# Two fused transformer blocks on one core: 256-column strips joined into 416 and 512 columns, a row statistic moved earlier, vector 6 turned one row sooner

## What is computed

```python
def first_block(x, c, ...):
    mod = (silu(c) @ w_ada + b_ada).reshape(b, 3, 3, D_MODEL)      # nine vectors of 1024
    x = x + 0.5 * mod[:, 0, 2] * swiglu(modulate(x, ...), w13[0], w2[0])
    h = modulate(x, norm_w[1], mod[:, 1, 0], mod[:, 1, 1])
    proj = h @ w_in                      # columns 0:416 are c_q (256), c_kv (128), k_rope (32)
    ...                                  # attention, convolution, two gated branches
    x = x + mod[:, 1, 2] * y
    h = modulate(x, norm_w[2], mod[:, 2, 0], mod[:, 2, 1])         # mod[:, 2, 0] is vector 6
    x = x + 0.5 * mod[:, 2, 2] * swiglu(h, w13[1], w2[1])
    return x

def second_block(x, ...):
    h = rmsnorm(x, norm_mix_g)
    z = h @ w_in                         # qa 1024, ka 256, va 256, qb, kb, vb 768 each, ga, gb
    y_a = mixer_a(qa, ka, va, ...)       # per head rmsnorm and rotation of q and k, softmax
    y_b = mixer_b(qb, kb, vb, rel_bias)
    x = x + (gate_a * y_a + gate_b * y_b) @ w_out
    ...                                  # squared-relu feed-forward, gated addition, last norm
```

## Time and profile before

| what | value |
|---|---|
| device time, median of 3 runs | 1023.25 us (1022.52 to 1025.52) |
| device time of the profiled execution | 1022.83 us |
| its span in the trace | 1021.0 us |
| TensorE busy | 1004.9 us (98%) |
| VectorE busy | 716.5 us (70%) |
| ScalarE busy | 536.9 us (53%) |
| HBM read | 209.88 MB, 207 GB/s over the span |

### The profile page before, as it was taken

The page is one execution under the profiler, slowest core; times in us unless marked ns, Lnnn a source line. Parts: engine busy times, 40 slices in busy tenths (PEclk is TensorE's granted clock), DMA queues, the critical chain, the costliest instruction groups (busy, mean ns, idle before and its releaser), DMA issues.

```text
span 1021.0 us, 19724 instructions
## 1 busy us (share of the span) xinstructions
PE 1004.9 (98%) x8440; PEld 983.6 (96%) x8440; DVE 716.5 (70%) x1234; ACT 536.9 (53%) x903; POOL 36.2 (4%) x71
## 2 busy tenths in 40 slices
PE   8999999999999999999999999999999999999997
PEld 6999999999999999999999999999999999999997
DVE  3587888978687787867665779655567775555586
ACT  4454444456656455544444577555456464444553
POOL 0121000000000010000000000004000000000000
PEclk9999999999999999999999999999999999999999
DMA  9979978956646673777646357446257565656521
GB/s 336 369 248 352 332 284 318 322 170 227 197 124 200 229 243 111 270 244 249 221 153 207 123 170 230 138 125 182 67 176 233 180 231 184 200 175 203 166 83 42
DMA packets 144479, 212.26 MB, mean 208 GB/s; under 512 B 4275, under 2 KB 121383, under 8 KB 144392
## 3 DMA queue, kind: packets, MB, share of 16 engines
q1 hardware_dynamic: 140032, 198.66, 58.2%
q0 software_dynamic: 4096, 12.10, 3.9%
q10 hardware_dynamic: 264, 0.25, 0.1%
HBM read 209.88 MB, written 1.11 MB: 207 GB/s over the span
## 4 chain that ended last, share of the span: by engine, by line
PE 89%; DVE 7%; ACT 2%; DMA 2%; issue 1%; SPq 0%; DVEq 0%
PE PS L471 87%; DVE wlo L1836 3%; PE PS L479 2%; DMA SC<-in_w_ada_dram 1%; DVE W L1778 1%; ACT whi L1329 1%; DVE hl L1787 0%; DVE xT L1787 0%; DMA SC<-in_x_dram 0%; DVE W L1787 0%; DVE SS L1778 0%; ACT W L1316 0%; ACT SR L1321 0%; DVE SR L1778 0%; ACT SC L1321 0%
## 5 line engine op out<-in xcount | busy, mean ns | idle before, releaser
L1836 DVE TENSOR_TENSOR wlo<-raw,whi 128x1024 fp32r<-128x1024 f32 (+2 forms) x331 | 386.3, 1186 | 151.8 <-ACT whi L1329 151.2
L1329 ACT ACTIVATE whi<-raw 128x1024 fp32r<-128x1024 f32 (+2 forms) x331 | 331.9, 1022 | 159.6 <-PE PS L471 129.5
L471 PE MATMUL PS<-hh,whi 128*128 128x256 f32 (+1 forms) x1376 | 391.7, 285 | 0.0
L471 PE MATMUL PS<-hh,wlo 128*128 128x256 f32 (+1 forms) x1376 | 387.6, 282 | 0.0
L471 PE MATMUL PS<-hl,whi 128*128 128x256 f32 (+1 forms) x1376 | 386.8, 281 | 0.0
L471 PE MATMUL PS<-SR,whi 128*128 128x256 f32 (+1 forms) x1824 | 328.6, 282 | 3.1 <-DVE xT L1787 1.6
L471 PEld LDWEIGHTS PS<-SR,whi 128*128 128x128 f32 x1824 | 279.9, 188 | 5.9 <-DVE xT L1787 2.4
L471 PEld LDWEIGHTS PS<-hh,whi 128*128 128x128 f32 x1376 | 259.1, 189 | 3.1 <-issue 2.2
L471 PEld LDWEIGHTS PS<-hl,whi 128*128 128x128 f32 x1376 | 260.2, 189 | 0.4
L471 PEld LDWEIGHTS PS<-hh,wlo 128*128 128x128 f32 x1376 | 260.0, 189 | 0.0
L471 PE MATMUL PS<-SR,wlo 128*128 128x256 f32 (+1 forms) x912 | 256.8, 282 | 0.0
(11 more groups left out here) (188 smaller groups left out, 741.2 us busy)
## 6 DMA issues: line engine op xcount, KB each, us to landing
raw<-in_ffn_w_dram SPq DMA_DIRECT2D x60, 1024.0 KB, 6.9
raw<-in_w_in_dram SPq DMA_DIRECT2D x38, 1024.0 KB, 5.5
raw<-in_w_ff_dram SPq DMA_DIRECT2D x32, 1024.0 KB, 5.3
raw<-in_w_ada_dram SPq DMA_DIRECT2D x20, 1024.0 KB, 6.8
SC<-in_w_ada_dram SPq DMA_DIRECT2D x8, 1024.0 KB, 11.1
SC<-in_w_ada_dram POOLq DMA_DIRECT2D x8, 1024.0 KB, 7.7
raw<-in_w_out_dram SPq DMA_DIRECT2D x8, 1024.0 KB, 5.1
raw<-in_ffn_w_dram SPq DMA_DIRECT2D x7, 768.0 KB, 10.4
```

What stands on the lines that cost most here:

```text
L471: return e.matmul(o, l, r, start=start, stop=stop, skip_group_check=True)
L1329: e.activation(hi_part(p), raw_part(p), ACT.Copy).then_inc(*hi_done.up(p.i))
L1836: e.tensor_tensor(lo_part(p), raw_part(p), hi32(hi_part(p)), ALU.subtract).then_inc(*lo_done.up(p.i))
```

## The change

1. `Plan.wider` is new: a load of four row blocks and n columns, in pieces of two row blocks. The strips of 256 and 160 columns of the first block become one strip of 416, and the six units of 256 columns of the second block three pairs of 512: qa, ka with va, qa. Each product of 128 tokens now takes one matmul per part and row block instead of two, and a pair takes two PSUM banks (6 and 7, 4 and 5, 6 and 7).
2. ScalarE reads a pair out as two units; ka and va are read before any of the second half of qa.
3. `token_sums` for key 2 moves from behind the first unit to the middle of the first pair. VectorE scales those sums (`token_mean`) as before, but now writes low parts between that and the reciprocal root.
4. `rstd_row(3)` stands behind the first pair, where it stood behind the second unit, with the same wait.
5. `last_columns` moves from behind row 5 to ahead of it, and ScalarE's copy of vector 6 ahead of its last high part of the branch sum.

```diff
@@ -169,6 +169,12 @@
         u = self.load(name, self.cols(w, c0, n, 0, kn), (kn, n))
         for k in range(0, kn, max(1, kn // 2)):
             self.piece(u, k, k + max(1, kn // 2), 0, n)
+
+    def wider(self, name, w, c0, n=512):
+        for q in (0, 4):
+            u = self.load(name, self.cols(w, c0, n, q, q + 4), (4, n))
+            for k in (0, 2):
+                self.piece(u, k, k + 2, 0, n)
 
     def tall(self, name, w, c0, kn=KD):
         u = self.load(name, self.cols(w, c0, 256, 0, kn), (kn, 256))
@@ -210,11 +216,7 @@
 
         for i in range(2):
             self.tall("gate", w_in, GATE0 + 256 * i)
-        c0 = self.load("c0", self.cols(w_in, 0, 256), (KD, 256))
-        c1 = self.load("c1", self.cols(w_in, 256, 160), (KD, 160))
-        for k in (0, 4):
-            self.piece(c0, k, k + 4, 0, 256)
-            self.piece(c1, k, k + 4, 0, 160)
+        self.wider("c", w_in, 0, CONV0)
         for i in (2, 3, 4):
             self.tall("gate", w_in, GATE0 + 256 * i)
         self.wide("uq", a["w_uq"][0], 0, 768, 2)
@@ -243,11 +245,9 @@
         self.row("r1", w2[1], NT - 2)
 
         QA, KA, VA, QB, KB, VB, GA, GB = (int(v) for v in np.cumsum([0, 1024, 256, 256, 768, 768, 768, 1024]))
-        for i in range(4):
-            self.wide("qa", w_in2, QA + 256 * i)
-            if i == 1:
-                self.wide("ka", w_in2, KA)
-        self.wide("va", w_in2, VA)
+        self.wider("qa", w_in2, QA)
+        self.wider("ka_va", w_in2, KA)
+        self.wider("qa", w_in2, QA + 512)
         for i in range(3):
             self.tall("qb", w_in2, QB + 256 * i)
         for i in range(3):
@@ -461,7 +461,7 @@
         back2 = [("qb", 0), ("qb", 1), ("qb", 2), ("kb", 0), ("kb", 1), ("kb", 2), ("vb", 0), ("vb", 1), ("vb", 2)] + \
                 [("gate2", i) for i in range(8)]
         back2_bank = [i % 3 for i in range(17)]
-        unit_bank = [6, 7, 4, 5, 6, 7]
+        pair_bank = (6, 4, 6)
 
         def pe_program(e):
             on = Wait(e)
@@ -727,14 +727,13 @@
 
             on.wait_ge(dve_done, ("x", 0, 6), ("x", 0, 7))
             for k in range(KD):
-                if k % 4 == 0:
-                    c0, c1 = take("c0"), take("c1")
+                if k % 2 == 0:
+                    p = take("c")
                 on.wait_ge(dve_done, (("h", 1), k))
-                for p, w, o in ((c0, 256, 0), (c1, 160, 256)):
-                    for t in range(2):
-                        m = mm3(PS[:, 2 + t, o:o + w], hx_tokens(k, t), halves(p, k % 4), k == 0 and o == 0, k == 7)
-                    if k % 4 == 3:
-                        m.then_inc(*count(("used", p.i), *(["c_rows"] if k == 7 and o else [])))
+                for t in range(2):
+                    m = mm3(PS[:, 2 + t, 0:CONV0], hx_tokens(k, t), halves(p, k % 2), k == 0, k == 7)
+                if k % 2 == 1:
+                    m.then_inc(*count(("used", p.i), *(["c_rows"] if k == 7 else [])))
             for q in (2, 3):
                 pair_rows(7, q, 0)
 
@@ -862,8 +861,9 @@
                         if j == 7:
                             last_rows()
                         row(j - 3)
+                        if j == 7:
+                            last_columns()
                         row(j - 2)
-                last_columns()
                 todo = [(take(name), aring[r % 4]) for r in (6, 7)]
                 on.wait_ge(dve_done, ("m", key, 7))
                 rows_end(todo, key)
@@ -952,31 +952,26 @@
 
 
             def by_token(n, name):
-                b = unit_bank[n]
-                if n < 4:
-                    on.wait_ge(dve_done, *((("mod", 8), ("u_in", 1, 20), ("u_in", 1, 21)) if n < 2 else (("u_in", 1, 21),)))
-                else:
-                    on.wait_ge(act_done, ("by_token", n - 4))
                 for k in range(KD):
-                    if k % 4 == 0:
+                    if n == 0 and k == 4:
+                        on.wait_ge(dve_done, ("x", 2, 7))
+                        token_sums(3, 2, True)
+                    if k % 2 == 0:
                         p = take(name)
                     on.wait_ge(dve_done, (("xs1", 2), k))
                     for t in range(2):
-                        m = mm3(PS[:, b, 256 * t:256 * t + 256], hx_tokens(k, t), halves(p, k % 4), k == 0 and t == 0, k == 7)
-                    if k % 4 == 3:
-                        m.then_inc(*count(("used", p.i), *([("by_token", n)] if k == 7 else [])))
-
+                        m = mm3(PS[:, pair_bank[n] + t, :], hx_tokens(k, t), halves(p, k % 2), k == 0, k == 7)
+                    if k % 2 == 1:
+                        m.then_inc(*count(("used", p.i), *([("by_pair", n)] if k == 7 else [])))
+
+            on.wait_ge(dve_done, ("mod", 8), ("u_in", 1, 20))
             by_token(0, "qa")
+            on.wait_ge(dve_done, ("spread", 2))
+            rstd_row(3, ("rstd_row", 3))
             on.wait_ge(dve_done, ("u_in", 1, 21))
-            token_sums(4, 2, True)
-            by_token(1, "qa")
-            on.wait_ge(dve_done, ("spread", 2), ("x", 2, 7))
-            rstd_row(3, ("rstd_row", 3))
-            on.wait_ge(dve_done, ("mean", 2))
-            by_token(2, "ka")
-            by_token(3, "qa")
-            by_token(4, "qa")
-            by_token(5, "va")
+            by_token(1, "ka_va")
+            on.wait_ge(act_done, ("by_token", 0), ("by_token", 1))
+            by_token(2, "qa")
             on.wait_ge(dve_done, ("keys2", 0), ("keys2", 1), ("x", 2, 6))
             for t in range(2):
                 for h in range(2):
@@ -1014,7 +1009,7 @@
                 for t in range(2):
                     b = 4 + 2 * hg + t
                     on.wait_ge(dve_done, ("queries2", hg, t))
-                    on.wait_ge(act_done, ("by_token", (2, 3, 4, 5)[2 * hg + t]))
+                    on.wait_ge(act_done, ("by_token", 2 + 2 * hg), ("by_token", 3 + 2 * hg))
                     for h in range(4 * hg, 4 * hg + 4):
                         m = turn(PS[:, b, 128 * (h % 4):128 * (h % 4) + 128], q2[:, t, 128 * h:128 * h + 128])
                     m.then_inc(*count(("qT2", hg, t)))
@@ -1043,7 +1038,7 @@
                 m.then_inc(*count(("pt2", n)))
 
             def values_a(h):
-                on.wait_ge(act_done, ("pt2", h), ("by_token", 5), *([] if h else [("qT2", 1, 1)]))
+                on.wait_ge(act_done, ("pt2", h), ("by_token", 3), *([] if h else [("qT2", 1, 1)]))
                 if h:
                     on.wait_ge(dve_done, ("oA", h - 1))
                 for kt in range(2):
@@ -1554,12 +1549,12 @@
                 for j in range(8):
                     hi_before(("stage", key, j))
                     opening(j)
+                    if j == 7 and last:
+                        last()
                     on.wait_ge(dve_done, ("mv", key, j))
                     if j >= 4:
                         on.wait_ge(mm_done, ("out_row", key, j - 4))
                     copy(aring[j % 4][0], W1[:, j % 3, 0:256], ("m_hi", key, j))
-                    if j == 7 and last:
-                        last()
                     hi_after(("stage", key, j))
 
             gated(1, lambda j: opened(j // 2 + 1, j // 2 + 5) if j % 2 and j < 7 else None, lambda: ada_rows_out(6, 4, 0, ("ada_sum", 6)))
@@ -1607,11 +1602,12 @@
 
 
             def by_token(n, dst, ss=None):
-                hi_before(("by_token", n))
-                on.wait_ge(mm_done, ("by_token", n))
+                hi_before(("by_pair", n // 2))
+                on.wait_ge(mm_done, ("by_pair", n // 2))
                 on.wait_ge(dve_done, ("rst", 2))
+                at = 256 * (n % 2)
                 for t in range(2):
-                    copy(dst[:, t, :], PS[:, unit_bank[n], 256 * t:256 * t + 256], ("by_token", n), scale=rst[:, t:t + 1])
+                    copy(dst[:, t, :], PS[:, pair_bank[n // 2] + t, at:at + 256], ("by_token", n), scale=rst[:, t:t + 1])
                 if ss is not None:
                     on.wait_ge(act_done, ("by_token", n))
                     for t in range(2):
@@ -1633,14 +1629,14 @@
             on.wait_ge(mm_done, ("rstd_row", 3))
             copy(RB[:, 0:S], PS[:, 3, 0:256], ("RB", 3))
             by_token(2, k2_, ss2[:, 0, :, :])
+            by_token(3, va)
             on.wait_ge(dve_done, ("head_rstd", 0))
             for t in range(2):
                 scaled_heads(k2_[:, t, :], 2, lambda h: st[:, 48 + 2 * t + h:49 + 2 * t + h], ("k_scaled", t))
-            by_token(3, q2[:, :, 512:768], ss2[:, 3, :, :])
             for t in range(2):
                 scaled_queries(0, t)
-            by_token(4, q2[:, :, 768:1024], ss2[:, 4, :, :])
-            by_token(5, va)
+            by_token(4, q2[:, :, 512:768], ss2[:, 3, :, :])
+            by_token(5, q2[:, :, 768:1024], ss2[:, 4, :, :])
             on.wait_ge(mm_done, "kT2")
             copy(kT2, PS[:, 2, :].rearrange("p (h c) -> p h c", h=2), "kT2")
 
@@ -2428,8 +2424,10 @@
                     if back2[m][0] == "gate2":
```

(8 more changed lines are left out.)

## The result

| what | before | changed |
|---|---|---|
| device time, median | 1022.73 us (1021.71 to 1025.52, 8 runs) | 1026.32 us (1025.44 to 1027.49, 8 runs) |
| profiled execution | 1022.83 us, span 1021.0 | 1025.97 us, span 1024.2 |
| TensorE busy | 1004.9 us | 1004.2 us |
| TensorE's matmuls | 8440 | 8248 |

The ratio is 1.0033, with a 95% interval of 1.0022 to 1.0044: slower by 3.4 us (2.2 to 4.5), just past what a measurement of this kernel tells from no change. The time lies in the predicted range, above the 1024.4 of the likeliest case and next to the 1026.5 of rival B.

A forecast was written before the change was run, and what follows sets the result against it. TensorE, busy 1004.9 of 1021.0 us, was taken as the bound. 1022.83 - 1.9 + 0.6 + 2.6 = 1024.1; that execution lay 0.4 below the median, so 1024.4 was predicted, range 1021.5 to 1027.5.

The forecast's parts named there:

- the likeliest case: The forecast itself for the whole kernel: 1024.4 us, its own range 1023 to 1025.5, chance 50%.
- rival B: TensorE's clock falls in the new gap of 4.2 us at the root: 1026.5 us, chance 20%.
- The 416 columns, -1.9: First block's joined strip: 48 matmuls at 0.190 us replace 96 taking 11.18 us; 1.9 us gained.
- Vector 6, +0.6: Vector 6 one row ahead: third high part lands behind ScalarE's `hh<-mod`, so x starts at 385.7, not 385.13.
- the wait forecast at 2.4 us: TensorE stands 2.4 us instead of 0.49 for vector 6's copy to HT, which is behind a high part.
- The idle time of 0.8 us: TensorE would idle about 0.8 us ahead of the fifth tile of `rows_end`, as a sign in the changed trace.
- The pairs and the root, +2.6: After the first pair TensorE waits 4.2 us for the spread behind six low parts; keys' transposes at 620.2, not 617.52.
- A: The forecast as summed for the whole kernel: 1024.4 us, range 1023 to 1025.5, chance 50%.
- B's price, +2.1: At the root's gap, a low clock lasting 4.1 us loses half of that: +2.1; at worst +11.
- C: No stall at the root, given at most two low parts ahead of it: 1018.9 us, chance 12%.
- Its -0.9 for vector 6: Lower bound at vector 6: HT comes in time and x a little sooner, 0.9 us gained.
- D: Second stall at the transposes of queries 4 to 7, +1 us: 1025.4 us, chance 10%; 1.3 us left otherwise.

The follow-up runs named there:

- e2: The kernel before with only the move of vector 6 (item 5); 1.0006 of the kernel before.
- e5: The changed kernel with 36 identity matmuls asked for in the gap ahead of the matmuls from `sm`, result overwritten; 1.0058 of the kernel before.
- e11: The changed kernel with three low parts ahead of the reciprocal root instead of six; 0.9984 of the kernel before.
- e7_vec6_early: The changed kernel with ScalarE's copy of vector 6 one row earlier too; 1.0038 of the kernel before.
- e8_both: The changed kernel with one low part ahead of the root and ScalarE's copy of vector 6 one row earlier; 0.9976 of the kernel before.
- e3_pairs: The kernel before with only the three pairs of 512 columns and items 2 to 4; 1.0046 of the kernel before.
- e6_four_low: The changed kernel with four low parts ahead of the root instead of six; 1.0006 of the kernel before.
- e12_after_again: The changed kernel as it is, measured and traced again; 1.0037 of the kernel before, median 1026.16 us.

## Why the prediction was right in its range and wrong in its likeliest case

**The 416 columns, -1.9:** -1.87 in the trace of that part alone, -2.1 by its time. The starts are 0.190 us apart, as the line between the two measured widths gave.

**Vector 6, +0.6:** the mechanism was as told (the third high part behind the copy to `hh`) and measures 0.5 to 0.7 at full clock; the wait forecast at 2.4 us was 2.25. What the sum left out is the clock: in four of the seven traces with a gap of 2.24 to 2.26 us it fell there (the changed kernel, `e2`, `e5`, `e11`), row 5 took longer, released the third high part's buffer later, and x came another 0.5 us later. The idle time of 0.8 us forecast ahead of the fifth tile of `rows_end` shows as about 1.0 where the clock stayed at full, and not at all where it fell: row 5 and the tiles behind it ended later, and filled it.

**The pairs and the root, +2.6:** a gap of 4.07 for 4.2 and six low parts ahead of the root, as forecast; the distance without the clock's part is +2.56. This term was right as it was written.

**Where the likeliest case failed** is the choice between A and B, the step "against it speaks that mine is at that edge, and that the longest gap inside the span before, 1.62 us, left the clock at full", with "it decides from a gap of about 4 us". The bound was read from the end of the span, from one fall after 4.1 us, as if the clock answered to the length of a gap alone. The runs show a fall behind gaps of 1.79 and 2.24 us. Between the 1.62 us that passed and the 4.1 us that did not lay all that was unknown, the forecast gap of 4.2 us lay above both, and B was the case to expect. And the 2.4 us stall that the prediction itself forecast at vector 6 was not priced for the clock at all. The Trainium skill (TensorE: Matmul & The Clock Gate, section on HAM oscillation) warns that TensorE falls to the lower clock in such a pause and pays for each; its own case is a wait for a DMA. At the root the traces agree: the clock fell behind all four gaps of 4.07 us, at 1.6 or 2.3 us. At vector 6, behind shorter gaps, it fell in four traces of seven, at 0.5 us.

**B's price, +2.1** for a low clock of 4.1 us whose half is lost, was 1.6 and 2.3 in the two traced executions. Added to the terms -1.87, +0.5 and +2.56 this gives +2.8 or +3.5, and 0.5 more with a fall at vector 6: 3.3 in the first profile by this sum, where the distances make 3.4. That the measured time stands so near B's 1026.5 is in part luck: in that profile the low clock made 2.1 us out of two falls of 3.4 us, one of them at a place that B doesn't name.

**C, 1018.9 with at most two low parts ahead of the root,** didn't come, but its condition fits and its price for the pairs was nearly right: with one low part the pairs gain 1.77 (1.5 forecast), and with three a gap of 0.67 us opens; two were not run. Its -0.9 for vector 6 never showed: where HT came in time, x was still 0.5 us late. So that the best kernel's 1018.66 stands next to 1018.9 is in part luck.

**D** didn't come: in the changed kernel the last rotation of queries 4 to 7 ends at 637.8, and TensorE starts their transposes at 639.11 without a wait. The 1.3 us left are those of the estimate.

The best version is the changed kernel with one low part ahead of the root and vector 6 left where it was: 0.9963 (0.9950 to 0.9975), 3.8 us faster than before and about 7.5 faster than the change as made.

## What to carry to other kernels

Joining strips made this TensorE-bound kernel faster (by 1.9 us at the 416 columns, and by 1.8 at the pairs once five of the six low parts were out of the way), but it also shortened the cover over a chain on another engine: when the work between a question and its answer is halved, count what stands ahead of the answer on that engine, and limit it to what fits. Price a new idle time of TensorE as the gap and the lower clock behind it, from the first gap that is longer than any which the trace shows to be harmless; a wait that costs nothing by itself can still cost the clock. Compare profiles by distances between marks around each edit, since the start of the program alone moved by more than an edit was worth.

## What the runs showed of the hardware that was not expected

- The same gap does not always do the same. Behind 2.24 to 2.26 us of idle time the clock fell in four traces and stayed at full in three; behind 2.15 us it stayed twice (`e7_vec6_early` and `e8_both`, ahead of the first x tile) and behind 2.01 us once; behind 1.79 us it fell once, and behind 1.60 to 1.62 us it stayed four times; behind 4.07 us it fell in four of four (the changed kernel twice, `e3_pairs`, `e7_vec6_early`). The times of `e2_vec6` fit this: its six executions with a mean clock of 0.996 took 1023.46 us on average, its five with 0.997 to 0.999 took 1022.85.
- It can fall when TensorE works again: at vector 6 0.9 us after the restart in the changed kernel and 0.5 after it in `e2_vec6`, at the root 1.2 after it in `e6_four_low` and 1.0 in `e3_pairs`. It can also fall within the gap, 1.8 and 1.9 us before the restart (`e7_vec6_early`, `e12_after_again`).
- A low stretch inside the span lasted 3.4 us seven times, each time that it began at or after the restart, and 6.8 us both times that it began within the gap (`e7_vec6_early`, `e12_after_again`), with TensorE busy all through its second half. Whether it is this that decides, the runs don't settle.
- The start of the 416 columns lay between 232.00 and 233.91 us from the start of the span over the fourteen traces, and the distance from the first x tile to the first unit or pair was either 195.9 or 196.3, in kernels with and without each edit. Neither was traced to a cause.
